# Seven products instead of eight for the up-projection, its squared rows kept in DRAM, and a new order of the gate operations

## The reference

```
m = W_out [ retention | HGRN2 | sliding-window attention ](x)
x = LayerNorm(ALPHA * x + m)
h = relu(x W_up)              W_up: 1024 x 4096
x = LayerNorm(ALPHA * x + (h * h) W_down)
```

## Time and profile before

| | |
|---|---|
| median of 3 runs | 2863.51 us (2863.49 to 2869.93) |
| the profiled execution | 2869.88 us, span 2868.1 |
| PE busy | 2653.6 us (93%), 17502 matmuls |
| PE weight loads busy | 2408.4 us (84%) |
| DVE / ACT / POOL busy | 1395.1 / 831.8 / 814.0 us |
| mean granted clock of PE | 0.961 |
| DRAM traffic | 182.66 MB read, 43.06 MB written |
| matmuls of the up-projection | 3 x 1536, 1492.4 us busy |
| matmuls of the down-projection | 3 x 1472 and 3 x 128 |

### The profile page before, as it was taken

The page is one execution under the profiler, slowest core; times in us unless marked ns, Lnnn a source line. Parts: engine busy times, 40 slices in busy tenths (PEclk is TensorE's granted clock), DMA queues, the critical chain, the costliest instruction groups (busy, mean ns, idle before and its releaser), DMA issues. The chain is left out here.

```text
span 2868.1 us, 42897 instructions
## 1 busy us (share of the span) xinstructions
PE 2653.6 (93%) x17502; PEld 2408.4 (84%) x17502; DVE 1395.1 (49%) x3036; ACT 831.8 (29%) x1692; POOL 814.0 (28%) x894
## 2 busy tenths in 40 slices
PE   6998888789999999999899988787989999999996
PEld 6997776588899999999899877666889999999996
DVE  2136668556434334343741466774563434343348
ACT  2235456322121212111122445561221121212120
POOL 0027456631212111111000455664311112121110
PEclk9999989889999999999999999996999999999998
DMA  4442213162111111110344431321621111111103
GB/s 155 142 148 86 83 60 90 40 188 85 59 45 45 45 59 45 45 45 30 100 141 141 143 96 53 102 66 27 195 97 45 45 45 45 45 45 45 59 23 107
DMA packets 182357, 226.48 MB, mean 79 GB/s; under 512 B 26256, under 2 KB 158672, under 8 KB 182128
## 3 DMA queue, kind: packets, MB, share of 16 engines
q1 hardware_dynamic: 182160, 223.73, 24.2%
HBM read 182.66 MB, written 43.06 MB: 79 GB/s over the span
## 5 line engine op out<-in xcount | busy, mean ns | idle before, releaser
L950 PE MATMUL ps<-u_hi,wu_hi 128*128 128x512 f32 (+2 forms) x1536 | 498.6, 325 | 0.0
L951 PE MATMUL ps<-u_lo,wu_hi 128*128 128x512 f32 (+2 forms) x1536 | 498.0, 324 | 0.0
L952 PE MATMUL ps<-u_hi,wu_lo 128*128 128x512 f32 (+2 forms) x1536 | 495.8, 323 | 0.0
L950 PE MATMUL ps<-hid_hi,wd_hi 128*128 128x256 f32 (+2 forms) x1472 | 475.4, 323 | 17.5 <-DVE acc_a L2431 7.2
L951 PE MATMUL ps<-hid_lo,wd_hi 128*128 128x256 f32 (+2 forms) x1472 | 473.4, 322 | 0.0
L952 PE MATMUL ps<-hid_hi,wd_lo 128*128 128x256 f32 (+2 forms) x1472 | 471.9, 321 | 0.0
L2399 DVE TENSOR_TENSOR relu<-relu 128x512 f32<-128x512 f32 (+2 forms) x192 | 102.8, 535 | 531.0 <-ACT relu L1871 531.0
L950 PEld LDWEIGHTS ps<-hid_hi,wd_hi 128*128 128x128 f32 x1472 | 278.5, 189 | 39.9 <-DVE acc_a L2431 7.8
L2691 POOL TENSOR_TENSOR wd_lo<-wd_raw,wd_hi 128x1024 fp32r<-128x1024 f32 x60 | 143.2, 2409 | 589.6 <-ACT wd_hi L1846 589.6
L952 PEld LDWEIGHTS ps<-u_hi,wu_lo 128*128 128x128 f32 x1536 | 290.3, 189 | 22.0
L950 PEld LDWEIGHTS ps<-u_hi,wu_hi 128*128 128x128 f32 x1536 | 289.4, 188 | 23.0
(11 more groups left out here) (274 smaller groups left out, 5417.5 us busy)
## 6 DMA issues: line engine op xcount, KB each, us to landing
wu_raw<-in_w_up SPq DMA_DIRECT2D x32, 1024.0 KB, 5.3
wd_raw<-in_w_down SPq DMA_DIRECT2D x32, 1024.0 KB, 4.8
wl_raw<-in_w_in SPq DMA_DIRECT2D x20, 1024.0 KB, 5.3
wi_raw<-in_w_in SPq DMA_DIRECT2D x15, 1280.0 KB, 6.4
out_y<-xn SPq DMA_DIRECT2D x32, 512.0 KB, 4.3
hscr<-h_out SPq DMA_DIRECT2D x80, 160.0 KB, 1.7
hb<-hscr SPq DMA_DIRECT2D x16, 512.0 KB, 4.1
xin<-out_y SPq DMA_DIRECT2D x16, 512.0 KB, 4.1
```

Of the source, the lines that this page charges most:

```text
L950: nc.tensor.matmul(out, a_hi, b_hi, start=start, stop=False)
L951: nc.tensor.matmul(out, a_hi, b_lo, start=False, stop=False)
L952: return nc.tensor.matmul(out, a_lo, b_hi, start=False, stop=stop)
```

## The change

**Up by seven products.** For the blocks 2 to 15 the up-projection is a product of 256 columns, 1024 inputs and 1056 rows. Each of the three is cut in two, and the four quarter results are made of seven products of quarter matrices and sums of them (PRODUCTS: four sums of weights S1 to S4, four sums of rows T1 to T4, in Winograd's order). The rows are cut into two sides, tokens 0 to 511 (twice 256) and 512 to 1055 (twice 272), with all seven products for each side: 14 products of 4 x 3 matmuls per block, in all eight banks in turn. Sums of rows are made once per layer: of side 0 on POOL (`side`, ten operations of 1024 elements and four subtractions, from the end of the output projection on), of side 1 on DVE (`side_t1` to `side_t4`, `side_low`), between the squares of the last six up units. Sums of weights are made per block on DVE. ACT rounds seven quarters per block, POOL makes the seven subtractions. DVE adds the products up out of PSUM, in 14 additions per block, then rectifies and squares both sides in one operation each.

**A phase of its own, rows in DRAM.** All 14 up blocks run first, then all down blocks. The squared rows of each block (256 x 1056) go to a DRAM tensor `hidscr` (`save_h`) and come back in the down phase (`load_hid`), where ACT rounds and DVE subtracts them one block ahead. A down block takes the token groups one after another, eight output tiles each. The rows' roundings and subtractions of blocks 0 and 1 leave the first up units.

**Gates.** `gates_clip` of chunk f moves from the end of the previous step into the middle of the step, after `front_levels`; the three functions of the clipped gates (`gates_out`) stand on ACT after place b, ahead of the second half of the window's exponentials; `front_silu` stands after `heads_merge`. The keys (`gates_keys`) are made at the end of DVE's step; the copy of the queries moves into `gates_log`, after `window_high`. On POOL the product of the gate with the norm weight (`gate_weights`) is the last of the prompt part of a step, and in step 4 `rotate` comes after `levels`. SP's waits are the same.

```
+PRODUCTS = (("W11", "U11"), ("S2", "T2"), ("W12", "U21"), ("S3", "T3"), ("S1", "T1"), ("W22", "T4"), ("S4", "U22"))
+SIDES = ((0, 256), (512, 272))
+            def load_quarters(l, b):
+                if b == 2:
+                    sp.wait_ge(wu_hi_done, 2 * (l + 1))
...
+                    sp.wait_ge(wq_lo_done, NPROD * n + product_of("W22") + 1)
+                    sp.wait_ge(ws_dve.sem, ws_dve.at("s4", n))
...
+            def load_hid(l, b, c):
+                if b == 0:
+                    sp.wait_ge(up_ready, product_done(l, FBLOCKS - 1, product_of("S3" if c else "S2"), 1))
+                elif b == 1:
+                    sp.wait_ge(up_ready, UPS * (l + 1))
+                else:
+                    sp.wait_ge(down_ready, down_no(l, b - 2, KT - 1, c) + 1)
...
+            def product(l, b, i, s):
...
+                for k in range(4):
+                    hi, lo = token_part(tokens, k, s)
+                    last = three(ps[:, bank_of(l, b, i, s), 0:SIDES[s][1]], wq_hi[weights][:, k, :], wq_lo[weights][:, k, :],
+                                 hi, lo, k == 0, k == 3)
...
+                for b in range(2, FBLOCKS):
+                    up(l, b)
                 for b in range(FBLOCKS - 2):
                     down(l, b)
-                    up(l, b + 2)
...
+            def up(l, b):                                    # DVE
...
+                for s in range(2):
+                    dve.wait_ge(xd.sem, xd.at(f"x3{s}", n))
+                    add("q22", s, "S1", quarter(s, 1, 1), u3[s][:])
+                    add("x4", s, "S1", u2[s][:], u2[s][:])
+                if b + 1 < FBLOCKS:
+                    weight_sums(l, b + 1)
+                else:
+                    hid_low(l, 0, 0)
...
+                        if (c, d) in ((1, 1), (1, 5), (2, 3)):   # in collect
+                            hid_low(l, b + 1, ((1, 1), (1, 5), (2, 3)).index((c, d)))
...
+                collect_last(l, 0, 0, 4)
+                for c in range(TCH):
+                    hid_low(l, FBLOCKS - 1, c)
+                collect_last(l, 0, 4, 8)
...
+            def side(l):                                     # POOL
...
+                pool.wait_ge(out_ready, 24 * (l + 1))
...
+                difference("t1", "12", "11")
+                less("t2", "22", "t1")
+                difference("t3", "22", "12")
+                less("t4", "21", "t2")
+                for m in ("T2", "T3", "T1", "T4"):
+                    pool.wait_ge(ta[0].sem, ta[0].at(m, l))
+                    g_.tensor_tensor(t_lo[0][m][:], raw[m][:], t_hi[0][m][:], ALU.subtract).then_inc(tp.step(f"l{m}"), 1)
...
                     dense(step, "b")                          # ACT, chunk step
+                    if f:
+                        gates_out(f)
                     if f and f.prompt:
                         window_exps(f, "B")
...
-                    if f:                                    # DVE, chunk step
-                        front_silu(f)
...
                         front_levels(f)
+                        gates_clip(f, chunk_at(l, step - 2))
...
                         heads_merge(h)
+                    if f:
+                        front_silu(f)
                     if f and f.prompt:
                         if g:
                             gates_sigmoid(g)
                         window_low(f)
-                        if g:
-                            gates_clip(g, h)
...
                         heads_low(h)
+                    if g:
+                        gates_keys(g)
```

More of the change, by code:

```diff
@@ L1422, in up @@
             def up(l, b):
-                for f in range(2):
-                    for c in range(TCH):
-                        up_unit(l, b, f, c)
+                for i in range(NPROD):
+                    for s in range(2):
+                        product(l, b, i, s)
             def down(l, b):
                 q = b % 2
[L1429 to L1434, removed]
+                hi, lo = wd_of[q]
@@ new lines, in side_high, with weight_high @@
+            def side_high(l, s, m):
+                S = (tp, tv)[s]
+                act.wait_ge(S.sem, S.at(m.lower(), l))
+                if s == 0 and m == "T4":
+                    act.wait_ge(nd.sem, nd.at("res", norm_no(l, 0, 7)))
+                copy(t_hi[s][m][:], t_raw[s][m][:]).then_inc(ta[s].step(m), 1)
+            def weight_high(l, b, i):
+                n, m = seven_no(l, b), PRODUCTS[i][0]
+                if m[0] == "S":
+                    act.wait_ge(ws_dve.sem, ws_dve.at(m.lower(), n))
+                else:
+                    act.wait_ge(wq_in, 16 * (n + 1))
+                act.wait_ge(up_ready, place_free(l, b, i))
+                copy(wq_hi[m][:], w_quarter(m)).then_inc(wq_hi_done, 1)
@@ L2087, in gates_sigmoid, with gates_keys @@
                     dve.wait_ge(gc.sem, gc.at("s", c.n))
+                    for j in range(2):
+                        v.scalar_tensor_tensor(out=g_r[:, j, :], in0=g_e[:, j, :], scalar=lb[:, j:j + 1], in1=g_r[:, j, :],
+                                               op0=ALU.mult, op1=ALU.add).then_inc(gc.step(f"f{j}"), 1)
+                def gates_keys(c):
                     dve.wait_ge(gp.sem, gp.before(c.n))
@@ L2091, in gates_sigmoid @@
                             .then_inc(gc.step(f"k{j}"), 1)
-                    for j in range(2):
-                        v.scalar_tensor_tensor(out=g_r[:, j, :], in0=g_e[:, j, :], scalar=lb[:, j:j + 1], in1=g_r[:, j, :],
-                                               op0=ALU.mult, op1=ALU.add).then_inc(gc.step(f"f{j}"), 1)
                 def gates_clip(c, h):
+                    dve.wait_ge(h_in[c.p], c.loads * 64)
                     if h:
@@ new lines, in side_t4, with side_low @@
+            def side_t4(l):
+                dve.wait_ge(y_out[1], y_stores(l, 0, 7))
+                raw = t_raw[1]["T4"]
+                v.tensor_tensor(raw[:], u_part(u_hi, "21", 1), t_raw[1]["T2"][:], ALU.subtract).then_inc(tv.step("t4a"), 1)
+                dve.wait_ge(tv.sem, tv.at("t4a", l))
+                v.tensor_tensor(raw[:], raw[:], u_part(u_lo, "21", 1), ALU.add).then_inc(tv.step("t4"), 1)
+            def side_low(l, m):
+                dve.wait_ge(ta[1].sem, ta[1].at(m, l))
+                v.tensor_tensor(t_lo[1][m][:], t_raw[1][m][:], t_hi[1][m][:], ALU.subtract).then_inc(tv.step(f"l{m}"), 1)
@@ L2653, in mix_step @@
                             split_wo(l, OUT_BEFORE[step])
-                    if g:
+                    if g and step != 4:
                         rotate(g)
```

493 lines of the change are left out of this document (360 added, 133 removed).

## The result

The changed kernel takes 2902.8 us (four runs, 2897.8 to 2904.28), the kernel before 2863.5 (four runs, 2861.42 to 2869.93): a ratio of 1.0133 with a 95% interval of 1.0114 to 1.0152. It is 39 us slower, where 2837, 26 us faster, was forecast. The profiled execution took 2904.21 us with a span of 2902.1; its mean granted clock is 0.944 against 0.961.

The account below looks back on a forecast made before the run. Feed-forward blocks were taken as bound by matmul rate, chunk steps by chains between engines. From 2869.88 us, -77.8 - 4.5 + 3 + 27 + 26 = -26, then 6.4 lower for the median: 2837; own range 2820 to 2856, with two rivals 2788 to 2866.

Parts of the forecast that it names:

- second rival: Costs of the gates and of the phase's start both at their upper ends, +40 each: 2864 us, no change; chance 0.12.
- the start of the phase: DVE's norms beside POOL's sums, and DVE's side sums: +13.5 us a layer, +27 for two (+10 to +40).
- Third: Rival: the weights' loop of load, sums, rounding and subtractions bounds the up phase; 3022 us with a loop of 27; chance 0.03.
- fourth rival: Weight loads set a floor, 256 and 272 columns both cost 0.1333 us a matmul, block 22.4: 2893 us; chance 0.02.
- Block 2: First up block by seven products: DVE's side sums run against the last six up units, +1.5 us a layer.
- Gates: New order of the gates in the chunk steps: +13 us a layer, +26 for two; bounds -5 and +20 a layer.
- Step 7: Chunk step where output weights stand behind SP's wait for the gate product and ACT waits for them: +9.7 us.
- Steps 1 and 2: Chunk steps where late weights leave 4.7 us later behind SP's wait, delaying PE's next levels: +3.8 and +4.4 us.
- End: End of the down phase: PE waits for three row subtractions on DVE, +1.5 us a layer, +3 for two.
- Norms: DVE's norms of tiles 4 and 5 alternate with POOL's sums at the phase's start: net +12 us a layer.
- Down blocks: Steady ones keep matmuls and widths, 23.2 us; waits of first down and last up block go, -4.5 us for both layers.
- Seven products: Up blocks take 20.4 us (19.7 to 21.1) against 23.18, 14 in each of 2 layers: -77.8 us.

## Why the prediction was wrong

It forecast a gain and the kernel became slower; the measured time lies beyond the range and beyond the second rival. That rival, both costs at their upper ends, came nearest: it had +40 for the gates, where 42.6 were measured, and +40 for the start of the phase, where 54.6 were. Third and fourth rival, the slower ones, did not happen: no loop of the weights bound the phase (PE has no gap in blocks 3 to 15), and 256 and 272 columns cost 0.118 and 0.126 us a matmul as taken. Of the 60 us between forecast and profiled execution:

- **Block 2, 20.3 us: the step that failed.** "The side sums of DVE itself then run against the last six up units; I charge +1.5 for the first block" sized a load of work and never followed a queue. It asked whether DVE was in time, not what stands behind DVE's late sum on ACT: the rectification that frees the bank. The run with that one instruction moved gave back 13.4 us, 11.3 of them in block 2. With this one term right the sum would still have missed: the two profiles would differ by +14 us, not -26.
- **Gates, 16.6 us: right mechanism, under-sized.** The wait of the SP queue, the load of late weights behind it in the steps of chunks 2 and 3, the loads of output weights in step 7 and ACT's 9.35 us wait for them ("some 10") are as forecast, and moving SP's waits gives back the whole loss. Step 7 was priced at 9.7 and lost 11.9 and 8.9 by the transposes of the heads; the forecast's own terms (512.9 + 2 + 3.2 to 5) give 518.1 to 519.9 and not its 520.6, so 7.2 to 9.0 instead of 9.7. Step 6, whose output weights the same wait delays, wasn't priced for it: 4.1 and 3.1. The clock's 5.2 in the samples' step were only in the upper bound. Steps 1 and 2 were priced at +3.8 and +4.4 and lost 7.4 and 7.2 at the level products. Two reasons can be read there, neither was tested by itself. The issue is late by 4.7 as forecast, but the load then takes longer: 6.5, 7.3 and 7.7 us for the three issued at 273.87, 300.62 and 329.16, where the same loads took 5.3, 7.1 and 6.2 before. And once `u_lo` is late, the keys (L2302), moved to the end of DVE's step, stand between it and g_kt. They run beside POOL's subtraction of 4.51 us (282.36), and the first of the two takes 2.95 us where it took 0.28 before. PE's chain of waits has them in:

```profile
273.87 6.50 DMA wl_raw<-in_w_in
...
282.80 0.69 DVE u_lo L2530
283.49 0.59 DVE u_lo L2537
284.09 3.55 DVE g_k L2302 x2
```

- **End, 8.3 us.** The three subtractions were seen (+1.5 a layer), but the last weights' subtraction beside them was not. It stood at the same place before (1368.66, 4.76 us, 1.9 after the last up block), where DVE was through with its rows at 1368.12; now the two hold each other, 5.7 us and 4.9. The clock's share comes on top: after the wait of 3.55 us PE ran 5 us at 0.50.
- **Norms, 7.3 us.** The alternation was forecast, and it came out strict: seven held operations lose some 2.2 us each, 15 in all, which is the forecast's +12 before its -3 is taken off. PE's waits grew by 12.9 and 12.1 us, as priced. Most of what is missing, 3.2 us a layer, is the clock: it is 0.50 from 695 to 710, and this was left out, as it was at block 2, where it is 0.50 from 765 to 770. But for the upper bound of the gates the prediction priced waits as if the work behind them ran at full speed. Over the four places (norms 6.4, block 2 3.3, end 5.4, samples' step 5.2) that is some 20 of the 60 us, an estimate from the stretches less their waits.
- **Down blocks, 4.9 us.** A steady one takes 23.36 against 23.23, without one gap over 0.25 us: PE's spacing is 0.5% longer on average, 3.6 us over the phase of both layers. The cause stays open. The other 1.2 are the first down block, 23.81, which kept part of its waits.
- **Seven products, 2.8 us**: 20.50 against 20.4, the one term that decided the forecast and was nearly exact.

The remaining 5 us between 2837 and 2902.8 are the profiled execution of before, 6.4 above its median, while that of after lies 1.4 above.

The length of a POOL operation is paid as often as DVE has instructions with two SBUF inputs in that stretch, tiny ones included: seven were held between 684 and 703.4. The Trainium skill (SBUF — State Buffer, the section "SBUF: two separate sides") has the loser wait for the other's whole instruction. The trace agrees: 2.3 us for an operation of 0.16 us.

## What to carry to other kernels

When a producer moves within a step, look up every queue that waits for it, and then what stands behind that wait: here a wait of SP that cost nothing at the start of a step made a new order of operations cost 45 us once its producer came at the end, and moving the wait down SP's list turned that into a gain of 8. Where DVE runs a chain of short operations with two SBUF inputs, cut POOL's operations short: here DVE paid for their length (0.7 instead of 2.3 us each time), though their sum grew. And follow a late result through each engine's order to the bank or buffer that it frees, with the half-speed clock after the wait in the price.

## What was not expected

- A wait of PE costs more than its length. After 13 us of waits (691 to 706) it runs at 0.50 until 710, after 10 us (758.8 to 768.9) at 0.50 until past 770, and after 3.55 us at 1390.73 also, until past 1395. The kernel before had it too, on a smaller scale: after 3.36 us of wait at 685.75 the clock is 0.67 from 685 to 690.
- A gap that the profile books as "issue" (10.03 us) was a wait for a rectification on ACT; only moving that instruction gave it its name.
- The longer the operations of the two engines that take turns, the worse for the one with the tiny ones: 0.16 us became 2.3 beside 2.36-us operations and 0.69 beside 0.73-us ones.
